# Loading two expert sums by blocks of 128 whole rows instead of by column quarters, with their additions shared between VectorE and GpSimd

## What is computed

```python
    out = lax.map(expert_block, ...)
    routed = jax.ops.segment_sum(out.reshape(rows, D), row_tok, num_segments=n_tok)
    ...
    x = x + gate2 * moe(h2, ...)
    ...
    h = x @ w_in        # first product of the second block, on the new x
```

## Time and profile before

| | |
|---|---|
| three runs, median (lowest to highest) | 2369.04 us (2365.80 to 2372.58) |
| the profiled execution, device time | 2366.73 us |
| its span, first to last instruction | 2364.9 us |
| mean granted TensorE clock | 0.987 of full |
| the sums' transfers (`YF`) | 8 x 512 KB, issued from 1102.31 us |
| stretch looked at | 1102 to 1130 us |

### The profile page before, as it was taken

The page is one execution under the profiler, slowest core; times in us unless marked ns, Lnnn a source line. Parts: engine busy times, 40 slices in busy tenths (PEclk is TensorE's granted clock), DMA queues, the critical chain, the costliest instruction groups (busy, mean ns, idle before and its releaser), DMA issues.

```text
span 2364.9 us, 30566 instructions
## 1 busy us (share of the span) xinstructions
PE 2258.3 (95%) x10242; PEld 1760.4 (74%) x10242; DVE 1538.0 (65%) x2360; ACT 1199.5 (51%) x1774; POOL 292.5 (12%) x248
## 2 busy tenths in 40 slices
PE   7998999899999999997999999999999789999997
PEld 5776566778888888874766788888788457888885
DVE  7789766899999999986654643333442766333344
ACT  4432434588888888874434332333222763322333
POOL 0000000343334334433000000000110000000000
PEclk9999999999999999999999999999999999999999
DMA  8511245799999999995210132233232001322232
GB/s 331 178 54 63 81 169 185 269 360 395 387 393 388 391 391 392 391 328 164 91 52 28 58 116 97 95 106 99 89 98 97 11 30 60 116 98 96 99 107 81
DMA packets 107472, 415.71 MB, mean 176 GB/s; under 512 B 20161, under 2 KB 32705, under 8 KB 82640
## 3 DMA queue, kind: packets, MB, share of 16 engines
q1 hardware_dynamic: 87408, 378.47, 42.7%
q0 software_dynamic: 19504, 34.73, 5.9%
q10 hardware_dynamic: 432, 0.87, 0.1%
HBM read 408.67 MB, written 43.65 MB: 191 GB/s over the span
## 4 chain that ended last, share of the span: by engine, by line
PE 77%; DVE 8%; ACT 5%; issue 5%; DVEq 2%; DMA 1%; POOLq 0%; SPq 0%; POOL 0%; ACTq 0%
PE PS L298 22%; PE PS L300 22%; PE PS L299 21%; ACT wh L192 3%; PE PS L714 3%; PE PS L2010 2%; PE PS L736 2%; DVE wl L197 1%; PE PS L725 1%; DMA ada_wa<-wada 1%; PE PS L2035 1%; DVEq L1285 1%; DVE M L1282 1%; PE PS L1245 1%; DVE HG L2075 0%
## 5 line engine op out<-in xcount | busy, mean ns | idle before, releaser
L197 DVE TENSOR_TENSOR wl<-raw,wh 128x1024 fp32r<-128x1024 f32 x239 | 292.5, 1225 | 357.2 <-ACT wh L192 351.0
L298 PE MATMUL PS<-HTh,wh 128*128 128x512 f32 x1248 | 498.6, 400 | 6.5 <-ACT V L881 2.2
L300 PE MATMUL PS<-HTh,wl 128*128 128x512 f32 x1248 | 486.9, 390 | 0.0
L299 PE MATMUL PS<-HTl,wh 128*128 128x512 f32 x1248 | 486.6, 390 | 0.0
L197 DVE TENSOR_TENSOR wl<-eraw,wh 128x1024 fp32r<-128x1024 f32 x384 | 457.5, 1219 | 16.7 <-ACT wh L192 13.5
L192 ACT ACTIVATE wh<-raw 128x1024 fp32r<-128x1024 f32 x239 | 252.0, 1056 | 362.7 <-PE PS L300 338.7
L192 ACT ACTIVATE wh<-eraw 128x1024 fp32r<-128x1024 f32 x384 | 392.6, 1054 | 17.4 <-PE PS L300 15.0
L298 PEld LDWEIGHTS PS<-HTh,wh 128*128 128x128 f32 x1248 | 234.4, 188 | 72.6 <-issue 13.4
L300 PEld LDWEIGHTS PS<-HTh,wl 128*128 128x128 f32 x1248 | 234.5, 188 | 49.9
L299 PEld LDWEIGHTS PS<-HTl,wh 128*128 128x128 f32 x1248 | 234.7, 188 | 49.7 <-issue 3.4
L298 PE MATMUL PS<-wh,XTh 128*128 128x512 f32 x536 | 221.1, 412 | 1.9 <-DVE wl L2195 1.4
(11 more groups left out here) (413 smaller groups left out, 3454.2 us busy)
## 6 DMA issues: line engine op xcount, KB each, us to landing
eraw<-wstream SPq DMA_DIRECT2D x192, 1024.0 KB
raw<-wstream SPq DMA_DIRECT2D x240, 512.0 KB, 3.3
ada_w<-wada SPq DMA_DIRECT2D x20, 512.0 KB, 5.7
eraw<-wexp SPq DMA_DIRECT2D x9, 1024.0 KB
ada_wb<-wada SPq DMA_DIRECT2D x2, 2048.0 KB, 15.6
ada_l<-wada SPq DMA_DIRECT2D x8, 512.0 KB, 3.4
ada_g<-wada SPq DMA_DIRECT2D x2, 2048.0 KB, 10.3
expert_sum<-LM SPq DMA_DIRECT2D x8, 512.0 KB, 5.4
```

The costliest lines, as they stand in the source:

```text
L197: nc.vector.tensor_tensor(wl[:, ci % RING, :], src, wh[:, ci % RING, :].bitcast(F32), ALU.subtract).then_inc(split_done, 1)
L298: nc.tensor.matmul(o, lh, rh, start=start, stop=False)
L299: nc.tensor.matmul(o, lh, rl, start=False, stop=False)
L300: return nc.tensor.matmul(o, ll, rh, start=False, stop=stop)
```

## The change

The two sums are loaded by blocks of 128 tokens: block tb of `ysum[s]` goes to `YF[:, s, tb, :]`, rows of 1024 floats (4 KB). There are still eight transfers of 512 KB, in the order block 0 of both sums, block 1 of both, and so on. DVE adds blocks 0 and 2, POOL blocks 1 and 3; each addition is still 128 x 1024. PE's turn of the very first tile (m = 0) now waits ahead of each of its four transposes for the addition of that block; later tiles need no wait for additions, since all blocks are there by then. `keep_clock(2)` between the first two turns is taken out.

```diff
-            YF = place("YF", [P, 2, 4, NB, 256], 3072)
+            YF = place("YF", [P, 2, NB, D], 3072)
...
-                for q in range(4):
+                for tb in range(NB):
                     for s in range(2):
-                        sp.dma_start(YF[:, s, q, :, :], ysum[s].rearrange("(b p) (q d) -> q p b d", p=P, q=4)[q]
-                                     ).then_inc(ya_in[q], 16)
+                        sp.dma_start(YF[:, s, tb, :], ysum[s].rearrange("(b p) d -> b p d", p=P)[tb]).then_inc(ya_in[tb], 16)
...
             def quarter_turn(pe, q):
-                if q:
-                    pe.wait_ge(sem("ya_whole"), q)
-                else:
-                    pe.wait_ge(sem("ya_first"), 1)
                 for m in (2 * q, 2 * q + 1):
                     if m >= 4:
                         pe.wait_ge(sem("ya_read"), m - 3)
                     for tb in range(NB):
+                        if m == 0:
+                            pe.wait_ge(*((sem("ya_first"), tb // 2 + 1) if tb % 2 == 0 else (sem("ya_whole"), tb // 2 + 1)))
                         mm = nc.tensor.transpose(PS[:, SUM_BANK[m % 4], tb * P:(tb + 1) * P],
-                                                 YF[:, 0, q, tb, m % 2 * P:(m % 2 + 1) * P], const("ident"))
+                                                 YF[:, 0, tb, m * P:(m + 1) * P], const("ident"))
...
-                dve.wait_ge(ya_in[0], 32)
-                nc.vector.tensor_tensor(YF[:, 0, 0, :, :], YF[:, 0, 0, :, :], YF[:, 1, 0, :, :], ALU.add).then_inc(sem("ya_first"), 1)
+                for tb in (0, 2):
+                    dve.wait_ge(ya_in[tb], 32)
+                    nc.vector.tensor_tensor(YF[:, 0, tb, :], YF[:, 0, tb, :], YF[:, 1, tb, :], ALU.add).then_inc(sem("ya_first"), 1)
...
-                for q in range(1, 4):
-                    pool.wait_ge(ya_in[q], 32)
+                for tb in (1, 3):
+                    pool.wait_ge(ya_in[tb], 32)
                     pool.sem_inc(passed_pool, 1)
-                    nc.gpsimd.tensor_tensor(YF[:, 0, q, :, :], YF[:, 0, q, :, :], YF[:, 1, q, :, :], ALU.add).then_inc(sem("ya_whole"), 1)
+                    nc.gpsimd.tensor_tensor(YF[:, 0, tb, :], YF[:, 0, tb, :], YF[:, 1, tb, :], ALU.add).then_inc(sem("ya_whole"), 1)
...
                 keep_clock(6)
                 quarter_turn(pe, 0)
-                keep_clock(2)
                 quarter_turn(pe, 1)
```

## The result

The changed kernel took 2374.83 us (median of 9 runs, 2372.24 to 2377.36) against 2368.88 for the kernel before (median of 9, 2365.80 to 2372.58): a ratio of 1.0027, 95% interval 1.0019 to 1.0035; the medians lie 6.0 us apart. In a second series it was 2372.96 against 2368.05, a ratio of 1.0020 (1.0010 to 1.0030). The forecast was 2374.0. The profiled execution took 2375.4, its span is 2373.6.

What follows compares the result with a forecast made beforehand. TensorE was taken to bound the kernel. First matmul at 1120.5, then a pair of 13.54 us less 0.6 (hole) plus 0.7 (clock), ends at 1134.1: +5.0 on the median 2369.04 gives 2374.0 us, range 2370 to 2379.5.

Steps and rivals of the forecast that it cites:

- Step 2: First tile of X: needs all four blocks, so it waits for load 8, not load 2; the cost of the edit.
- Step 1: Loads of the sums: 4 KB rows land 1.25 us apart, the last near 1114.6 instead of 1117.9.
- rival A: Loads of the sums: 4 KB rows land no sooner, last at 1117.9; +8.3 us, 2377.3; chance 0.17.
- Step 3: Additions of the sums: POOL's for block 3 ends last, taking 2.35 us, at 1117.15.
- Step 4: TensorE's transposes: 13 of the first 16 come behind block 3's addition; first low part at 1119.7, TensorE free at 1118.8 or 1120.5.
- Step 5: DVE's low parts of X: the 4.6 us stall beside POOL's additions goes, worth only 0.6 us.
- the hole: TensorE's 0.6 us wait before 1121.25, in the next linear's first pair of units, for DVE's low part of X.
- Step 6: TensorE without keep_clock(2): lower clock at 1117.2, back about 1121.9; first matmul +0.8, matmuls at half speed +0.7 us.
- Rivals B and C: TensorE's clock: B, stays down through the first pair, +7.4 us, chance 0.09; C, never falls, +3.5 us, chance 0.09.
- Step 7: SP's issues and queues: weight loads behind the sums land by about 1118.4 instead of 1121.7; worth nothing.

Runs made afterwards that it cites:

- both side costs out: Changed kernel with warming matmuls between tile 0's transposes and DVE, not POOL, adding blocks 1 and 3: ratio 1.0016 to the kernel before, mark (third unit's first matmul) 31.53 us.

## Why the prediction was right

The forecast was +5.0 us, the two series gave +6.0 and +4.9. By its steps, all from the first issue, with the second profile of the changed kernel beside the first:

- **Step 2, who must be there: right**, and the largest part. First matmul at 20.5 and 19.6 us for a forecast of 18.2, where 13.3 was before; with both side costs out the mark is still 4.4 late, and with half of the late bytes the gap between the layouts is half.
- **Step 1, row length: the mechanism was right, a term of the sum was mis-sized.** I took the last landing at 12.3 (3.3 + 7 x 1.25 + 0.2); by issue and time to landing it was 14.9 and 14.0, and 13.6 to 14.4 in five other kernels with these rows, for 15.4 to 15.9 in three with 1 KB rows. The spacing nearly held (2.6 and 2.7 for a pair in the changed kernel's two profiles, forecast 2.5); the start did not, as 3.3 us was the median of all weight loads and not the start of such a queue. The 4 KB rows are worth about 1.6 us on the mean of these profiles, not 3.3; no run changed the row length alone. That is half of rival A, whose own ground, the tensor just written, is ruled out by the run with another source. The Trainium skill's 358 GB/s (SBUF — State Buffer, as cited in the prediction) gave a landing at about 13.7, close to the measured one, but for another reason: windows of the pure 4 KB rows show 415 and 420 GB/s, over the page's figure. What lowers the mean, as far as the windows show, is the slow start and the part of the bytes that already belongs to the weight loads behind.
- **Step 3, additions: right.** 2.33 us for POOL's last, undisturbed; exchanging the engines gave back 1.1, what the 2.33 less 1.23 says.
- **Step 4, transposes: right in place**, 13 behind the last block, 2.95 us at the lower clock (forecast 2.9).
- **Step 5, port stall: right.** 5.4 us for eight low parts (forecast 5.5). That it was worth only the hole was nearly so: taking it away alone, with quarters, gave 1.4 us, about half of it by the earlier start.
- **Step 6, the clock: right**, with a cost of about 1 us measured for 1.5 forecast. It fell between 1113 and 1114; it returned 2.7 and 3.9 us after the transposes resumed, ahead of my 4.7. Rivals B and C fell.
- **Step 7** cost and brought nothing visible. The weight loads behind landed 17.7 and 18.7 us behind the first issue, not the forecast's 16.1 (19.4 before), and no engine waited for them.

So the last landing was 1.7 to 2.6 us later than I said, and the earlier return of the clock made up for part of it. The mark was at 33.6 and 33.2 where the sum gives 32.2 (the pair's end at 31.8 and 0.35 to the next unit), a loss of 6.5 and 6.0 for the forecast 5.0. That the second series came out at +4.9 is therefore luck in part: the prediction named a delay that is made good later as a sign of being wrong, and in the second profile 1.5 us of it are made good behind the mark, near 1210, where the kernel before spent 3.4 us at the lower clock and this run none. The first profile lost about 1 us there instead.

## What to carry to other kernels

When a producer finishes late, count the bytes that stand between its end and the consumer's first piece: cut transfers along what the consumer takes first, not along what makes the longest rows; 4 KB rows won about 1.6 us here, and the change still lost over 4 with the clock held and the last block on the faster engine. Give the piece that arrives last to the faster engine, and keep GpSimd's additions away from VectorE operations with two SBUF operands. Warming matmuls that look idle may be holding the clock: read the granted clock behind them before taking them out. Loads moved ahead of a late indirect transfer are no gift: beside it they cost what they won; over before it started they won 2.2 us in one layout and nothing in the other.

## What the runs showed of the hardware that was not expected

- Eight loads of 512 KB issued at once, in 4 KB rows: the first lands after 4.1 to 4.4 us, where the median weight load needs 3.3, and the first pair is whole after about 6 (7.2 in one profile).
- A large load from SP's queue beside an indirect addition of POOL's: it landed after 6.7 us instead of 5.1, and the next step of POOL came 5.0 instead of 2.5 us later. An indirect addition in the middle of the overflow blocks landed after 8.9 and 9.7 us beside such loads, and after 5.9 to 7.2 in the twelve other profiles.
- The return of the clock took from 2.7 to 3.9 us after the transposes resumed in the same kernel, so one profile doesn't price it.
